# Second stage's x tiles two by two in seven half products: token sums made once and streamed through the ring

## The reference, cut to what matters

```python
proj = m @ p['w_in']                                     # (256, 2048) @ (2048, ...)
xbc = silu(centred_dwconv(proj[..., OFF_X:OFF_DT], ...)) # x (4096 columns), B (1024), C (1024)
# ssd_context_states: the same x and B columns for the context, to get the start states
xb = silu(centred_dwconv(m_ctx @ w[:, OFF_X:OFF_C], ...))
```

## Time and profile before

| | |
|---|---|
| median of three runs | 3456.13 us |
| the profiled execution, its own time | 3457.11 us |
| its span | 3455.3 us |
| PE busy in the span | 3200.0 us (93%) |
| DVE, ACT, POOL busy | 1851.0, 525.4, 918.8 us |
| mean granted TensorE clock | 0.96 of full |
| DMA | 989.40 MB, mean 286 GB/s |

### The profile page before, as it was taken

One profiled execution on the slowest core, in us unless ns is written; L12 is line 12 of the kernel. 1 busy time (PEld: TensorE's weight loads), 2 busy tenths in 40 slices (PEclk: granted clock), 3 DMA queues, 4 the chain that ended last, 5 costly groups with the idle time before them and its releaser, 6 DMA issues. The chain is left out here.

```text
span 3455.3 us, 30801 instructions
## 1 busy us (share of the span) xinstructions
PE 3200.0 (93%) x10108; PEld 1775.5 (51%) x10108; DVE 1851.0 (54%) x3355; ACT 525.4 (15%) x1056; POOL 918.8 (27%) x618
## 2 busy tenths in 40 slices
PE   6999999999999999999999999998987887878876
PEld 2467667575857576777644444443433333333332
DVE  6544444444444344666756434656566566565655
ACT  2312212121212121211000001111111111111110
POOL 0011112020202111100000002555555555555553
PEclk8999999999999999999999999999998898898988
DMA  9764554545463645545554597999999999999997
GB/s 359 288 227 179 188 185 175 200 169 209 149 231 132 231 163 205 205 170 192 200 180 170 171 342 296 398 427 423 427 421 423 423 426 424 426 427 427 426 427 311
DMA packets 152449, 989.40 MB, mean 286 GB/s; under 512 B 17771, under 2 KB 30764, under 8 KB 38572
## 3 DMA queue, kind: packets, MB, share of 16 engines
q0 software_dynamic: 73728, 536.90, 37.0%
q1 hardware_dynamic: 67104, 424.88, 33.9%
q10 hardware_dynamic: 11536, 26.55, 2.0%
HBM read 969.13 MB, written 19.14 MB: 286 GB/s over the span
## 5 line engine op out<-in xcount | busy, mean ns | idle before, releaser
L2535 PE MATMUL ps<-gates,diagonal 128*128 128x512 f32 x2048 | 992.2, 647 | 198.6 <-ACT diagonal L2163 198.6
L1075 PE MATMUL ps<-mT,ring 128*128 128x256 f32 (+1 forms) x4096 | 1168.9, 446 | 1.1 <-PEq L216 1.1
L1075 PEld LDWEIGHTS ps<-mT,ring 128*128 128x128 f32 x4096 | 775.0, 190 | 387.9 <-issue 318.2
L2352 DVE CUSTOM_DVE_ANT_0 u_rows<-u_rows,yhy 128x2048 f32<-128x2048 f32 x256 | 585.9, 2292 | 470.4 <-DMA u_rows<-in_peer_u_dram,expert_index 458.3
L2535 PEld LDWEIGHTS ps<-gates,diagonal 128*128 128x128 f32 x2048 | 420.5, 208 | 768.7 <-issue 637.9
L2096 POOL DMA_INDIRECT gates<-in_peer_v_dram,expert_index x256 | 418.9, 1636 | 502.8 <-PE ps L2535 417.3
L2096 POOL DMA_INDIRECT u_rows<-in_peer_u_dram,expert_index x256 | 273.6, 1069 | 135.8 <-issue 134.6
L707 POOL TENSOR_TENSOR dd<-mask_f,dt_g 128x1024 f32<-128x1024 f32 x16 | 30.3, 1896 | 933.0 <-DVE dt_g L977 932.4
L867 DVE SCALAR_TENSOR_TENSOR conv<-ps,tap_g,conv 128x510 f32<-128x510 f32 (+1 forms) x48 | 33.8, 704 | 338.7 <-ACT conv L728 338.7
L2157 ACT ACTIVATE gelu<-dot 128x4 f32<-128x4 f32 x64 | 13.1, 205 | 1059.2 <-DVE dot L2352 1059.2
L881 DVE SCALAR_TENSOR_TENSOR ada_sums<-ada_tiles,csil,ada_sums 128x1024 f32<-128x1024 f32 x120 | 153.9, 1283 | 4.0
(11 more groups left out here) (372 smaller groups left out, 2878.2 us busy)
## 6 DMA issues: line engine op xcount, KB each, us to landing
ring<-in_w_stream_dram SPq DMA_DIRECT2D x160, 1024.0 KB, 5.0
ada_tiles<-in_w_ada_dram SPq DMA_DIRECT2D x64, 1024.0 KB, 6.8
ring<-in_w_mix_dram SPq DMA_DIRECT2D x48, 1024.0 KB, 4.9
ring<-in_w_mod_dram SPq DMA_DIRECT2D x32, 1024.0 KB, 10.7
ring<-in_w_out_dram SPq DMA_DIRECT2D x32, 1024.0 KB, 5.4
rows<-cum_rows_scratch SPq DMA_DIRECT2D x16, 1536.0 KB, 13.1
ring<-in_w_q_dram SPq DMA_DIRECT2D x11, 1024.0 KB, 7.2
hf_scratch<-hf ACTq DMA_DIRECT2D x8, 768.0 KB, 6.4
```

The source lines that it names most:

```text
L1075: mm = nc.tensor.matmul(ps[:, k % 4, 0:n], m.ring[:, slot, kt * P:(kt + 1) * P], m.mT[:, kt, 0:n], start=(kt == 0), stop=(kt == KT - 1))
L2352: nc.vector.tensor_tensor_reduce(out=u_slot[n], in0=u_slot[n], in1=h2[:, t, :], scale=1.0, scalar=0.0, op0=ALU.mult, op1=ALU.add, accum_ou ...
L2535: return nc.tensor.matmul(ps[:, 4 * t + b, :], dia[:, (h % 2) * S + n, :], v_slot[n][:, b * CH:(b + 1) * CH], start=first and n == 0, stop ...
```

## The change

The four x tiles of a group are done as two pairs. A pair is a 2x2 block product: the two weight tiles are the columns, the two halves of the contraction (8 tiles of 128 each) the rows; tokens and context are the two column blocks. Seven products of half the contraction by 256 columns replace the eight that the plain form has (Strassen's scheme in Winograd's form). Each has 8 matmuls.

- Token sums: four combinations of the quarters of `m.mT`, [128, 2048] each, depend on no weight. POOL makes them once, at the start of the block (`add_token_sums`, four subtractions of 2048 columns); SP stores them to a DRAM scratch tensor `token_sums`; the fourth waits for the store of the first, whose buffer it reuses. For every pair they are streamed through the ring as if they were weight tiles, so a pair has 6 turns instead of 2 and a group 24 turns instead of 16 (`GROUP_TURNS`).
- Weight sums: DVE makes them for each pair (`add_weight_sums`, four operations on 1024 columns, one of them in place in the ring).
- Joins: ACT copies the first product, DVE adds the rest into `xT` (`join_first`, `join_rest`: seven operations on 256 columns for a pair). Middle tap and side taps then read `xT`, not PSUM.
- Order: DVE does the ada quarters after turns 0 and 1 and after each pair; SP loads a pair of ada tiles after turns 18 (for the next group), 1, 5 and 9. In the first group SP first does the four stores, and `rows` is loaded after turn 5 and no longer after turn 3. PE turns the decays after the first pair of the first group (before: after turn 3).

The diff, cut to its core:

```diff
 # sync
-                def group(g, head):
-                    for k in range(GROUP_TILES):
-                        sp.wait_ge(m.w_used, g * GROUP_TILES + (START_B + k + 1))
-                        ... load turn k + 4
-                        if k == 0 or 2 <= k < 5:
-                            n = 2 * (k - 1) if k else 0
-                            ... wait ada_used, load two ada tiles
-                        if head and k == 3:
+                def group(g, head, last):
+                    for k in range(GROUP_TURNS):
+                        sp.wait_ge(m.w_used, g * GROUP_TURNS + (START_B + k + 1))
+                        s, turn = k % RING, k + RING
+                        at = turn - 2
+                        if at < PAIRS * PAIR_TILES and at % PAIR_TILES >= 2:
+                            n = at % PAIR_TILES - 2
+                            if head and at < PAIR_TILES:
+                                sp.wait_ge(tsum_st[n], 16)
+                            src = d.token_sums[n]
...
+                        sp.dma_start(m.ring[:, s, :], src).then_inc(m.w_full[s], 16)
+                        if k in (1, 5, 9):
+                            n = 2 + 2 * (k // 4)
+                            sp.wait_ge(ada_used, 16 * g + 2 * n)
+                            load_ada(g, n)
+                        if k == HY_TURN and not last:
+                            sp.wait_ge(ada_used, 16 * g + 16)
+                            load_ada(g + 1, 0)
+                        if head and k == 5:
                             sp.wait_ge(dt_st, 16)
                             load_rows(g)
                         if not head and k == 0:
                             sp.wait_ge(y_mm, XTILES * g)
                             load_rows(g)
+                load_ada(0, 0)
+                for n, at, src in ((1, T1_AT, tsum1), (2, T2_AT, tsum2), (3, T4_AT, tsum4), (4, T3_AT, tsum3)):
+                    sp.wait_ge(tsum_p, n)
+                    store_sum(at, src)
 # gpsimd, before its loop over the groups
+                    nc.gpsimd.tensor_tensor(tiles(tsum1), b12, b11, ALU.subtract).then_inc(tsum_p, 1)
+                    pool.wait_ge(tsum_p, 1)
+                    nc.gpsimd.tensor_tensor(tiles(tsum2), b22, tiles(tsum1), ALU.subtract).then_inc(tsum_p, 1)
+                    pool.wait_ge(tsum_p, 2)
+                    nc.gpsimd.tensor_tensor(tiles(tsum4), tiles(tsum2), b21, ALU.subtract).then_inc(tsum_p, 1)
+                    pool.wait_ge(tsum_st[T1_AT], 16)
+                    nc.gpsimd.tensor_tensor(tiles(tsum3), b22, b12, ALU.subtract).then_inc(tsum_p, 1)
 # vector
+                def add_weight_sums(g, i):
+                    first, second = 2 + PAIR_TILES * i, 3 + PAIR_TILES * i
+                    ... wait for both weight tiles
+                    nc.vector.tensor_tensor(wsum3, a11, a21, ALU.subtract).then_inc(wsum_v, 1)
+                    v.wait_ge(wsum_v, done + 1)
+                    nc.vector.tensor_tensor(a21, a21, a22, ALU.add).then_inc(wsum_v, 1)
+                    v.wait_ge(wsum_v, done + 2)
+                    nc.vector.tensor_tensor(wsum2, a21, a11, ALU.subtract).then_inc(wsum_v, 1)
+                    v.wait_ge(wsum_v, done + 3)
+                    nc.vector.tensor_tensor(wsum4, a12, wsum2, ALU.subtract).then_inc(wsum_v, 1)
+                def join_first(g, i):
+                    v.wait_ge(p1_a, 2 * g + i + 1)
+                    nc.vector.tensor_tensor(xT[:, 2 * i, 0:T], p1[:], ps[:, 2, T:2 * T], ALU.add).then_inc(join_v, 1)
+                def join_rest(g, i):
+                    v.wait_ge(m.w_used, used - 1)
+                    ... three additions (joins 2 to 4)
+                    v.wait_ge(m.w_used, used)
+                    ... three more (joins 5 to 7)
 # vector, group
-                    for ci in range(2 + XTILES):
-                        s = 1 if ci == 1 else 2
-                        side_taps(g, ci, ci, conv[...], s)
-                        if ci >= 2:
-                            ada_products(g, 2 * (ci - 2), head)
+                    for ci in range(2):
+                        side_taps(g, ci, ...)
+                        if ci == 0:
+                            add_weight_sums(g, 0)
+                        ada_products(g, 2 * ci, head)
+                    for i in range(PAIRS):
+                        join_first(g, i)
+                        join_rest(g, i)
+                        if i == 0:
+                            add_weight_sums(g, 1)
+                        for ci in (2 + 2 * i, 3 + 2 * i):
+                            side_taps(g, ci, xT[:, ci - 2, :], ...)
+                        ada_products(g, 4 + 2 * i, head)
 # tensor
+                def project_pair(g, i, head):
+                    x0 = await_tile(pe, m, START_B, turn, GROUP_TURNS, g)
+                    bank_free(2, -2, 2)
+                    product(ps[:, 2, 0:T], weights(x0, 0), tokens(0, 0))
+                    product(ps[:, 2, T:2 * T], weights(x0, half), tokens(half, 0)).then_inc(x_pe, 1)
+                    x1 = await_tile(pe, m, START_B, turn + 1, GROUP_TURNS, g)
+                    t4 = await_tile(pe, m, START_B, turn + 2 + T4_AT, GROUP_TURNS, g)
+                    pe.wait_ge(wsum_v, 8 * g + 4 * i + 4)
+                    bank_free(3, -1, 7)
+                    product(ps[:, 3, 0:T], weights(x1, half), token_sum(t4)).then_inc(used, 1)
+                    t1 = await_tile(pe, m, START_B, turn + 2 + T1_AT, GROUP_TURNS, g)
+                    product(ps[:, 3, T:2 * T], weights(x1, 0), token_sum(t1)).then_inc(used, 3)
+                    bank_free(0, 0, 4)
+                    product(ps[:, 0, 0:T], summed(wsum4), tokens(half, T))
+                    t2 = await_tile(pe, m, START_B, turn + 2 + T2_AT, GROUP_TURNS, g)
+                    product(ps[:, 0, T:2 * T], summed(wsum2), token_sum(t2)).then_inc(used, 1)
+                    t3 = await_tile(pe, m, START_B, turn + 2 + T3_AT, GROUP_TURNS, g)
+                    bank_free(1, 1, 6)
+                    product(ps[:, 1, 0:T], summed(wsum3), token_sum(t3)).then_inc(used, 1)
```

More of the change, by code:

```diff
@@ L51 @@
 GROUP_TILES = 1 + 1 + XTILES + XTILES + 6
+PAIRS = XTILES // 2
+PAIR_TILES = 2 + 4
+GROUP_TURNS = 1 + 1 + PAIRS * PAIR_TILES + XTILES + 6
+Z_TURN = 2 + PAIRS * PAIR_TILES
+HY_TURN = Z_TURN + XTILES
+T4_AT, T1_AT, T2_AT, T3_AT = range(4)
 GATE_TILES = 2 * KT
@@ L1077, in project, with product, weights, summed @@
                     mm.then_inc(m.w_used, 1)
+                def product(out, weight, tokens):
+                    for kt in range(KT // 2):
+                        mm = nc.tensor.matmul(out, weight(kt), tokens(kt), start=(kt == 0), stop=(kt == KT // 2 - 1))
+                    return mm
+                def project_pair(g, i, head):
+                    turn, joined, used = 2 + PAIR_TILES * i, 14 * g + 7 * (i - 1), m.w_used
+                    half = KT // 2
+                    def weights(slot, k):
+                        return lambda kt: m.ring[:, slot, (k + kt) * P:(k + kt + 1) * P]
+                    def summed(sums):
+                        return lambda kt: sums[:, kt * P:(kt + 1) * P]
+                    def tokens(k, lo):
+                        return lambda kt: m.mT[:, k + kt, lo:lo + T]
+                    def token_sum(slot):
+                        return lambda kt: m.ring[:, slot, kt * T:(kt + 1) * T]
+                    def bank_free(n, taps_of, joins):
+                        if i:
+                            pe.wait_ge(join_v, joined + joins)
+                        elif taps_of >= 0 or not head:
+                            pe.wait_ge(conv_v, 24 * g + 2 * taps_of + 2)
+                    x0 = await_tile(pe, m, START_B, turn, GROUP_TURNS, g)
[16 more added lines that the diff above has]
+                    product(ps[:, 1, 0:T], summed(wsum3), token_sum(t3)).then_inc(used, 1)
@@ L1106, in group @@
                 def group(g, head, last):
[L1107 to L1113, removed]
+                    for k in range(2):
+                        if not head:
                             pe.wait_ge(conv_v, 24 * g + 2 * k - 6)
                         project(g, k)
-                        if head and k == 3:
+                    for i in range(PAIRS):
+                        project_pair(g, i, head)
+                        if head and i == 0:
                             turn_decays()
+                    for k in range(6, GROUP_TILES - 2 if last else GROUP_TILES - 1):
+                        if k < 10:
+                            pe.wait_ge(join_v, 14 * g + (9, 14, 11, 13)[k - 6])
+                        elif k < 14:
+                            pe.wait_ge(zdone, XTILES * g + k - 9)
+                        else:
+                            pe.wait_ge(conv_v, 24 * g + 2 * (k - 8) + 2)
+                        project(g, Z_TURN + k - 6)
                         if k == 6:
@@ L2619 @@
     "cum_rows": (P, 3 * P),
+    "token_sums": (4, P, KT * P),
     "u_hy": (GROUPS, 6, P, T),
```

128 lines of the change are left out of this document (94 added, 34 removed).

## The result

The changed kernel takes 3469.89 us (median of 5 runs, 3467.32 to 3474.12) where the kernel before, timed beside it, takes 3456.13 (5 runs, 3453.86 to 3458.06): 1.0043 times as long, 95% interval 1.0028 to 1.0058. It is slower by 13.8 us, more than the 0.2% that a measurement can tell. The forecast was 3449, faster; the time fell inside the whole range and outside the forecast's own (3438 to 3460).

The account below looks back on a forecast made before the run. PE bounds the second stage, busy 200 of 200 us. First group +23.2 and seven later groups -30.4 sum to -7.2: 3457.1 becomes 3449.9, the median 3449; range 3422 to 3474, the forecast's own 3438 to 3460.

Parts of the forecast that it names:

- The seven products: PE, each pair: seven products of 3.455 us replace two wide tiles, saving 6.55 us a group, 52.4 in eight.
- The first group: First of eight groups: saving 6.55 us, but stalls and lower clock added, net +23.2 us.
- gaps of 13.7, 1.7, 7.5 and 2.0: First group, PE waits in us: weight sums 13.7, second ring tile 1.7, second pair's token-sum tile 7.5, z 2.0.
- 2.4 twice for the clock: First group: 2.4 us for lowered PE clock behind the weight-sum stall, and 2.4 behind the second pair's ring stall.
- z's stall: Every group, first z tile: four MiB queued in SP's loads land at 71.0, PE wants z at 69.0: 2.0 us.
- DVE's edge: Second pair's weight sums: ready 51.3, due 51.7, 0.4 us to spare; a rival (chance 0.22) had them up to 1 us late.
- -6.55 + 2.0 + 0.2 = -4.35: Each later group, in us: arithmetic saved, stall at z, late ring tile in the second pair; seven groups give -30.4.
- T4' at 41.4: 51.8, due 51.7: SP's queue, later group: second pair's token-sum tile, issued 41.4, lands 51.8, PE's product P3' wants it 51.7; cost 0.2 us.
- the edges go wrong: Rival: weight sums and T4' each up to 1 us late, z's stall sometimes lowers the clock; 3466 us, chance 0.22.
- the slower case: Rival: SP's queue at 2.75 us a MiB, T4' 3.0 late, z 2.8 late, 1 us of clock; 3484 us, chance 0.14.
- 11 us of hold: First group: DVE's decay steps held by POOL's token sums, weight sums 11 us later; ends 0 and 18.
- 12.9 (held): First group, if one-source DVE steps are held too: the product of 160.16 starts at 173.1, 12.9 us late.

Follow-up runs that it names:

- experiment 2: Changed kernel with both `rows` loads (3 MiB) moved after turn 12 in every group: 3459.64 us, ratio 1.0012.
- experiment 7: Kernel before the change, with POOL's four token sums added but not used: 3457.48 us, one run.
- experiment 1: Changed kernel with a group's last pair of ada tiles loaded after turn 15, behind z's two tiles: 3448.85 us, ratio 0.9977.
- experiment 3: Changed kernel with `rows` loaded after turn 12 and the last ada pair behind z's two tiles: 3431.42 us, ratio 0.9929.
- experiment 5: Changed kernel with `rows` after turn 12, the last ada pair behind z's tiles and the third ada pair after turn 7: 3423.71 us, ratio 0.9906.

## Why the prediction was wrong

What it had right. The seven products: 3.45 us each, 6.55 a group, measured 6.59. The first group: +23.2 forecast, +25.4 measured, with gaps of 13.7, 1.7, 7.5 and 2.0 forecast and 14.08, 1.34, 8.80 and 2.19 measured, and 2.4 twice for the clock (2.5 and 2.3). The cause of each was the one named (for T4' experiment 2 shows it: 8.8 became 1.2). The place and size of z's stall: 2.0 forecast, 2.2 measured. DVE's edge, feared in the rivals, held; the last of the four weight sums in the second group of the changed kernel:

```profile
388.08 1.22 DVE L983 TENSOR_TENSOR sq<-ring,dd 128x1024 f32<-128x1024 f32 x1
```

The sums are ready at 389.3, PE wanted them at 338.17 + 51.7 = 389.9.

**The step that failed** is the sum of a later group, "-6.55 + 2.0 + 0.2 = -4.35", in two places. One is its last term, from "T4' at 41.4: 51.8, due 51.7. This is on the edge; 0.2 us": it measured 1.3 a group, 9.2 in seven. The other is that a gap's lower clock and its restart have no term in it, and the prediction gives no reason (its rivals name the clock, not the restart): they measured 8.5 in seven groups. With both, and z 0.2 longer, the seven groups gained 12.6 and not 30.4, less than the first group lost. SP's queue of the changed kernel in that group, by issue:

```profile
352.10 0.33 SPq L701 DMA_DIRECT2D ring<-token_sums_scratch  x1
352.71 0.88 SPq L676 DMA_DIRECT2D rows<-cum_rows_scratch  x2
359.00 0.33 SPq L701 DMA_DIRECT2D ring<-token_sums_scratch  x1
364.19 0.87 SPq L682 DMA_DIRECT2D ada_tiles<-in_w_ada_dram  x2
369.36 3.78 SPq L701 DMA_DIRECT2D ring<-token_sums_scratch  x2
373.38 0.94 SPq L701 DMA_DIRECT2D ring<-in_w_stream_dram  x2
376.36 1.03 SPq L682 DMA_DIRECT2D ada_tiles<-in_w_ada_dram  x2
379.72 19.73 SPq L701 DMA_DIRECT2D ring<-token_sums_scratch  x4
```

The landing of the transfer issued at 379.72:

```profile
ring<-token_sums_scratch SPq DMA_DIRECT2D x1, 1024.0 KB, 11.9
```

T4 lands 4.8 after 352.10, at 356.9; T4' at 391.6. From the one to the other the queue lands 13 MiB (the 12 that the prediction counts, and T4' itself), always with more in it: 34.7 / 13 = 2.67 us each. The forecast had T4 at 18.8 and T4' at 51.8, so 33.0 for the same 13, 2.54 each, and T4' at 338.17 + 51.8 = 390.0. The issue times of the two agree to 0.2 (13.9 and 41.4 after the group's start forecast, 13.9 and 41.5 measured), so it is the rate. Of the 1.7 us that it was short, 1.3 arose in `rows`, whose 3 MiB took 8.9 where 7.6 were forecast. That, on an edge, became 0.8 to 1.9 us in each of seven groups, 9.2 in all.

The rest of a later group's difference (-4.35 forecast, -1.8 measured, 2.55 us): P3' 1.1 more than the 0.2, z 0.2 more, the clock 0.7, the restarts 0.5. The last two had no term in the later groups, though the first group had one for the clock. Over seven groups this is 17.8, with the first group's 2.2 it makes 20.0; less the 0.9 by which the stage starts earlier it is 19.1 of the 20.0 us between 3449.9 and 3469.89.

So the right case was the rival "the edges go wrong" (3466), in its T4' and clock and not in its weight sums. Its neighbour, the slower case, was to decide from 2.65 us a MiB, with T4' 3.0 late at 2.75; the queue ran at 2.67 and T4' was at most 1.9 late. The two were one quantity, the queue's rate, and the forecast put one value of it on an edge where an error can only add.

The weight sums of the first group: 11 us of hold were taken between 8.3 (one-source steps free) and 12.9 (held). They are held, 3.59 and 4.62 us for what takes 0.43, and yet it is 11.7, not 12.9, as the DVE view of the changed kernel shows (its first taps come at 187.79 instead of 176.99, in a stage that began 0.9 earlier):

```profile
158.36 3.59 DVE L1015 TENSOR_SCALAR w<-w 128x512 f32<-128x512 f32 x1 [1.07 <-ACT w L835]
161.98 4.62 DVE L1017 TENSOR_SCALAR w<-w 128x512 f32<-128x512 f32 x1
166.64 0.69 DVE L1019 TENSOR_TENSOR w<-w 128x512 f32<-128x512 f32 x1
167.25 5.01 DVE L1020 TENSOR_TENSOR w<-w 128x512 f32<-128x512 f32 x1
```

At 166.3 POOL has to wait for the store of the first sum, and a product (0.69) gets through in the pause; the next one is held in its place. So the pause isn't what takes 1.2 off the 12.9: experiment 7 has no pause, and the same 11.7. The prediction let the product of 160.16 start only behind all of POOL's work, at 173.1. In experiment 7 it is the step that stands under POOL's last operation (to 172.01), and it ends at 172.56. The rule of the Trainium skill (SBUF — State Buffer, the section "SBUF: two separate sides") is that a step of DVE with two SBUF inputs (beside a GpSimd operation that reads SBUF), or a tensor_scalar in a 2-port mode, shuts GpSimd out of the shared ports for its whole length or is shut out, whichever starts first. It was right here in both parts: L1015 and L1017 are float32 tensor_scalars, L1020 has two inputs. What was wrong in the 12.9 is the count of steps, not the rule.

What stays open. Why a gap of 2 us lowers the clock in one group and not in the next (three of 14 in the changed kernel, six of the eight at z in experiment 2) wasn't settled. Nor why `rows` goes slower than the rest: its 3 MiB took 8.9 us (2.97 each), the ten behind it 25.8 (2.58 each). The cost of the gaps at z and P3' is shown by experiments 1, 2, 3 and 5; that the clock fell behind some of them and not behind others is only what the traces record.

## What to carry to other kernels

A load that is added to a busy queue in order makes every load behind it later (here by some 2.6 us a MiB), so write down for each load when it is wanted, and put what is wanted late behind what is wanted soon: here the same bytes in another order were worth 4.8 us of a 157 us group, where the change as it stood had gained 1.8. Where a forecast finds a load "on the edge", it has a one-sided error, and the rate has to be worked out for the longest unbroken stretch of the queue; each gap that results also costs a restart (here 0.24) and now and then the clock (1.7). And a saving that repeats in a loop need not be taken in the first pass, where its inputs are still being made.

## What the runs showed of the hardware

- DVE's tensor_scalars on float32 SBUF tensors (512 columns, 0.43 us alone) took 3.6 and 4.6 us beside POOL's 2048-column operations. Not every one-source step is held: the reciprocal of experiment 2 took 3.35 beside POOL, as in the changed kernel, where POOL was idle. In experiment 2 the race for a pause fell the other way. There POOL resumed at 167.18 (and took 5.00 instead of 4.61); DVE's second product had started at 167.11 and took 0.68 instead of 5.01, and PE's gap at P3 was 10.6 instead of 14.1. So 3.5 us hung on whether that product started 0.07 ahead of POOL or, as in the changed kernel, 0.15 behind it.

```profile
167.11 0.68 DVE L1017 TENSOR_TENSOR w<-w 128x512 f32<-128x512 f32 x1
```

- Behind idleness of 1.9 to 2.8 us PE's granted clock was 1.00 in some places and 0.57 to 0.67 in others, and a narrow tile took 7.14 or 8.83 us.
- In a full queue a MiB took 2.67 us over 13 MiB (changed kernel, second group), and 4.6 to 4.9 alone.
